# Products of constants in the waits of TensorE, in a two-block kernel on one core

## What is computed

```python
# first block: 16 experts of width 512, each row goes to its best two
g_idx = top_k(softmax(xt @ rg_w + rg_b), 1)          # router 1
v, e_idx = top_k(expert logits of that group, 2)
y += comb[:, e:e+1] * ((silu(xt @ e_gate[e]) * (xt @ e_up[e])) @ e_down[e])
x = rms_norm(x + y, norm_f_g)                        # the join of the two blocks

# second block: 16 experts of width 2048, each expert picks its best 64 rows
probs = softmax(h @ w_router); gate, idx = top_k(probs.T, 64)     # router 2
xs = h[idx]                                          # gather
y = (silu(xs @ w_gate) * (xs @ w_up)) @ w_down * gate
out = rms_norm(x + segment_sum(y, idx), final_g)
```

## Time and profile before

| | us |
|---|---|
| median of 3 runs | 2079.98 (2079.97 to 2083.10) |
| profiled execution, its own time | 2081.55 |
| span of the profiled execution, first to last instruction | 2080.1 |
| TensorE busy in the span | 1863.6 (90%) |
| VectorE, ScalarE busy | 491.8, 272.3 |
| mean granted clock of TensorE | 0.965 |

### The profile page before, as it was taken

The page is one execution under the profiler, slowest core; times in us unless marked ns, Lnnn a source line. Parts: engine busy times, 40 slices in busy tenths (PEclk is TensorE's granted clock), DMA queues, the critical chain, the costliest instruction groups (busy, mean ns, idle before and its releaser), DMA issues.

```text
span 2080.1 us, 19253 instructions
## 1 busy us (share of the span) xinstructions
PE 1863.6 (90%) x8342; PEld 750.9 (36%) x8342; DVE 491.8 (24%) x978; ACT 272.3 (13%) x478; POOL 33.9 (2%) x44
## 2 busy tenths in 40 slices
PE   8999999979999969999995999988888888888886
PEld 4444444443333325545443333322222223222222
DVE  3566001241001026990124011111011111110112
ACT  3322000121010114402201100000000000000001
POOL 0000000010000010000000000000000000000000
PEclk9999999979999989999997999999999999999999
DMA  6221032456998881211256899999999999999996
GB/s 235 81 81 41 0 121 81 179 192 259 387 389 348 372 304 68 82 41 61 95 212 263 328 428 428 428 428 427 428 427 428 427 428 428 428 428 427 427 428 278
DMA packets 68537, 589.80 MB, mean 284 GB/s; under 512 B 5472, under 2 KB 6880, under 8 KB 37216
## 3 DMA queue, kind: packets, MB, share of 16 engines
q1 hardware_dynamic: 59904, 556.55, 64.8%
q10 hardware_dynamic: 4448, 17.28, 2.1%
q0 software_dynamic: 4096, 14.68, 2.1%
HBM read 575.91 MB, written 12.58 MB: 283 GB/s over the span
## 4 chain that ended last, share of the span: by engine, by line
PE 55%; DMA 36%; DVE 6%; issue 2%; ACT 1%; SPq 0%; POOL 0%; ACTq 0%; DVEq 0%
PE ps L252 23%; DMA ring<-in_w_up 21%; DMA ring<-in_w_down 9%; PE ps L2175 8%; PE ps L1032 7%; DMA ring<-in_exp_w_up 5%; PE ps L2201 5%; PE ps L661 3%; PE ps L1820 3%; PE ps L261 2%; PE ps L583 1%; PE ps L1712 1%; PE ps L2157 1%; DMA AR<-h_rows,AR 1%; PE ps L276 0%
## 5 line engine op out<-in xcount | busy, mean ns | idle before, releaser
L252 PE MATMUL ps<-AR,ring 128*128 128x512 f32 x1160 | 503.3, 595 | 4.9 <-DVE AR L2033 3.6
L252 PEld LDWEIGHTS ps<-AR,ring 128*128 128x128 f32 x1160 | 220.5, 191 | 280.7 <-issue 275.9
L2175 PE MATMUL ps<-ring,AR 128*64 128x512 f32 x1008 | 233.5, 607 | 43.8 <-DMA ring<-in_w_up 32.0
L1032 PE MATMUL ps<-ring,AR 128*32 128x512 f32 x1536 | 257.9, 623 | 12.6 <-DMA ring<-in_exp_w_up 10.0
L2313 DVE TENSOR_TENSOR XT<-XT,ps 128x512 f32<-128x512 f32 x128 | 82.0, 684 | 785.0 <-PE ps L2157 785.0
L2175 PE MATMUL ps<-AR 128*64 128x512 f32 x1040 | 235.2, 597 | 33.1 <-DMA AR<-in_w_up 23.5
L1032 PE MATMUL ps<-AR 128*32 128x512 f32 x768 | 164.2, 593 | 0.0
L2175 PEld LDWEIGHTS ps<-ring,AR 128*64 128x64 f32 x1008 | 69.1, 138 | 205.2 <-issue 119.7
L2175 PEld LDWEIGHTS ps<-AR 128*64 128x64 f32 x1040 | 71.6, 136 | 188.8 <-issue 120.7
L2201 PE MATMUL ps<-ring,AR 128*64 128x512 f32 x512 | 122.9, 628 | 6.7 <-DMA ring<-in_w_down 5.9
L1032 PEld LDWEIGHTS ps<-ring,AR 128*32 128x32 f32 x1536 | 72.5, 114 | 140.8 <-issue 140.3
(11 more groups left out here) (350 smaller groups left out, 1040.1 us busy)
## 6 DMA issues: line engine op xcount, KB each, us to landing
AR<-in_w_gate SPq DMA_DIRECT2D x33, 2048.0 KB, 33.6
ring<-in_w_up SPq DMA_DIRECT2D x32, 2048.0 KB, 35.4
AR<-in_w_up SPq DMA_DIRECT2D x32, 2048.0 KB, 33.5
ring<-in_w_down SPq DMA_DIRECT2D x32, 2048.0 KB, 35.4
AR<-in_w_down SPq DMA_DIRECT2D x32, 2048.0 KB, 35.4
ring<-in_w_gate SPq DMA_DIRECT2D x31, 2048.0 KB, 33.9
ring<-in_w_in SPq DMA_DIRECT2D x15, 2048.0 KB, 8.3
ring<-in_exp_w_up SPq DMA_DIRECT2D x15, 2048.0 KB, 13.7
```

What stands on the lines that cost most here:

```text
L252: x = PE.matmul(ps, l, r, start=i == 0, stop=i == len(pairs) - 1)
L1032: yield k, c, PE.matmul(b[32 * c:32 * c + 32, :], rows(k), w(k), start=k == 0, stop=k == nk - 1, tile_position=(0, 32 * c), skip_group_che ...
L2175: x = PE.matmul(GU[2 * m + f // 2][64 * (f % 2):64 * (f % 2) + 64, :], XS[n // 2 % 2][:, k * P + 64 * b:k * P + 64 * b + 64], w[:, kk_, f ...
```

## The change

A helper `idle_products(ps, n)` is added. It runs n products of the identity by 384 columns of constants into a PSUM bank. Nobody reads the result, and the bank's next user overwrites it. The helper is called at five places of TensorE's program, with 3, 7, 8, 14 and 7 products. No wait, no other engine's work and no load is changed.

```diff
+        def idle_products(ps, n):
+
+            for i in range(n):
+                PE.matmul(ps[:, 0:384], ident, con[:, 0:384], start=True, stop=True)
@@ pe_front
             for h in range(2):
                 gain_rows("gf", h, bank[x_bank(6 + h)])
 
+            idle_products(bank[x_bank(4)], 3)
             PE.wait_ge(s_rv, V_MSK)
@@ pe_few
             index(0)
             index(1)
+            idle_products(bank[f_bank["r1", 0]], 7)
             rows(0)
@@ pe_mixer2
+            idle_products(bank[7], 8)
             turn(0)
@@ pe_choice
             x.then_inc(s_cp, 1)
+            idle_products(DN, 14)
 
             PE.wait_ge(s_cv, V2_IF)
@@ pe_choice
             PE.wait_ge(s_cv, V2_ID)
+            idle_products(DN, 7)
             rows(0)
```

## The result

| | before | after |
|---|---|---|
| median of 20 runs each | 2080.29 us (2078.26 to 2083.10) | 2073.96 us (2068.13 to 2082.87) |
| ratio, 95% interval | | 0.9969 [0.9962, 0.9977] |
| profiled execution, its own time | 2081.55 | 2073.95 |
| span | 2080.1 | 2072.6 |
| mean granted clock | 0.965 | 0.977 |

The ratio, taken from the means, says that the change makes the kernel 0.31% or 6.4 us faster (4.8 to 7.9 by the interval); the medians are 6.3 us apart. The forecast was 2074.0.

A forecast was written before the change was run, and what follows sets the result against it. The last stream of loads waits for TensorE to free a slot, so TensorE time won before 1186 us counts. Gains of 2.8 and 3.2 us, 6.0 off the 2079.98 us median, give 2074.0 us, range 2071.3 to 2078.5.

The forecast's parts named there:

- The sum: Gains of the five calls added: 0 + 2.8 + 0 + 0 + 3.2 = 6.0 us.
- What bounds the kernel: Last load stream, after a hole, waits for TensorE to free a slot; only TensorE time won before 1186 us counts.
- The cost of a product: Each 384-column product takes 0.65 us at full clock, 1.30 at half; the clock rises after 4.4 to 5.2 us.
- 3 products before the mask: Hidden by TensorE's wait before the mask, with little gained behind: 0 us, bounds 0 to 0.4.
- 7 at the first gather: Before the first block's rows(0): 3.28 us of faster work less 0.5 of lateness, 2.8 us won.
- 8 at the join: They end about 3 us before turn(0), likely losing the clock again: 0 us, bounds 0 to 2.0.
- the join's case: Rival: turn(0) at the join runs at full clock, winning 2.0 us more, 2072.0 us; chance 0.07.
- 14 at the second router: After its transposes, hidden by 1 us in the wait for VectorE: 0 us, perhaps full clock for the next call.
- 7 at the second gather: Before the second block's rows(0): 3.47 us of faster work less 0.3 of lateness, 3.2 us won.
- The clock falls again: Rival: clock lost between filler and dense products at one or both gathers, 2076.2 to 2078.8 us; chance 0.15.
- Nothing: Rival: the products do nothing for the clock, or their gain is taken up elsewhere: 2080 us; chance 0.10.
- Slower: Rival: the clock doesn't rise and the products outlast their waits, 10.9 us lost, 2090.9 us; chance 0.05.

The follow-up runs named there:

- e1: Changed kernel with only the 7 products ahead of the first block's rows(0), the other four calls removed: 2076.38 us, ratio 0.9976.
- e2: Changed kernel with only the 7 products ahead of the second block's rows(0), the other four calls removed: 2077.39 us, ratio 0.9982.
- e3: Changed kernel with only the two calls of 7 products, one at each gather: 2075.57 us, ratio 0.9975.
- e4: Changed kernel with only the 14 products after the second router's transposes: 2079.45 us, ratio 0.9993.
- e6: Changed kernel with products of 16 instead of 384 columns, same calls and places: 2079.68 us, ratio 0.9998.
- e11: Changed kernel measured once more, no edit: 2074.53 us, ratio 0.9976.
- e5: Changed kernel with 14 instead of 8 products at the join: 2070.52 us, ratio 0.9952.
- e9: Changed kernel plus 2 products ahead of up_a in pairs 2 to 7 of the first block's experts: 2067.14 us, ratio 0.9935.
- e7: Changed kernel with 14 products at the join, plus 4 before the first norm's sums and 5 before the second mixer's second ga tile: 2070.64 us, ratio 0.9949.
- e8: Changed kernel with 28 instead of 14 products after the second router's transposes: 2077.05 us, ratio 0.9988.
- e10: Changed kernel plus 2 products before up_a (pairs 2 to 7), 4 before the first norm, 14 at the join, 9 at the second gather: 2065.45 us, ratio 0.9929.

## Why the prediction was right, and where it wasn't

**The sum.** 6.0 us were forecast and 6.4 measured (4.8 to 7.9). That the median came within 0.1 us of the forecast is luck: the two places give 2.9 + 2.6 = 5.5 us over all traces, and what nobody changed moves by more than the difference, as the points show.

**What bounds the kernel.** Right. All 7.5 us of the profile are won ahead of the load that closes the hole; behind it 878.30 and 878.31 us.

**The cost of a product.** Right: at full clock 14 instructions take 4.78 us, 0.68 a product against the estimated 0.65. The rise took 4.3 and 5.1 us after the start, and 3.9 to 5.4 over all traces of the wide filler at the gathers, near the 4.4 to 5.2. It doesn't hold at the join: without filler the clock rose 4.4 us after `turn(0)` started in the trace of before, and 7.9 to 9.5 us after in e1, e2, e3, e4 and e6. "Every dense stretch in the rows rose within 5.2 us" was right for the rows of one trace only.

**3 products before the mask.** 0, as forecast, as far as it can be told: e1 and e3, without them, have 22.00 and 22.10 us at the first gather, the seven traces with them 21.91 to 22.52. The forecast had the clock full when they start; in the profile after it had fallen at 443.2 us, before them, and was back at 446.6.

**7 at the first gather.** 2.85 us in the profiles against 2.8, 2.9 over thirteen traces. The faster work behind the filler is worth 3.29 us against the forecast's 3.28. The 0.5 us of lateness is the lucky part: the filler was not late in the profile after, but the gathered rows landed 0.44 us later than in the profile before (11.62 against 11.18 us after the mask). In the six traces where the filler ended last, `rows(0)` came 0.05 (e1) to 0.7 us (e11) later than in the profile of before.

**8 at the join.** The reason was right: they end too early, and `turn(0)` took 3.42 us against the "close to 3.77". The stage of the join won 0.87 us in the profiles, within the bounds of 0 to 2.0, and 0 over all traces. e5 shows what the forecast called the join's case when the filler reaches to the work; there it is worth 3.1 us, more than the 2.0 that the row of before gave. The forecast took it that a gap of 3 us would cost the clock: here it was 3.5 us long and did cost it, 3.0 us in; but e5's clock held over 3.58 us at the gating. Such a gap may go either way.

**14 at the second router.** They were hidden by 1.1 us against the 1 forecast, and brought nothing alone (e4). The full clock for the next call, which the forecast hoped for, was there in the profile after and gone in e5, e9 and e11.

**7 at the second gather.** Forecast 3.2 us, in the profiles 1.70 + 2.55 = 4.25, and another 1.70 at the down instructions, where the fall of the earlier trace rows is gone; over all traces 2.6. Two terms of the step were off in size. The 0.3 us of lateness wasn't there in this trace, because the 14 had left the clock high, and the gather landed 1.0 us sooner (6.72 us after the index products against 7.69); in e11, of the same kernel, the filler was last and `rows(0)` came after 8.43 us. And the 2.59 us were too much: the first 64 instructions take 15.4 to 16.9 us in the four traces without filler (mean 16.1) and 14.15 on the mean of the nine with it, which is 1.9 us. The trace of before was the slowest of the four over the whole place, so the profile's gain of 5.95 is more than twice what the place gives on the mean. The forecast's 3.2 lies between the two.

**What the forecast left out.** Stretches in which nothing was changed moved by -0.35, +0.83 and +1.63 us. Falls of the clock at other places move such stretches, and the third is one of them. Before router 2 there are 16 instructions of 512 columns whose chain rows are, in the profile before and after,

```profile
1108.38 6.98 PE ps L1820 x16
```

```profile
1105.08 8.67 PE ps L1828 x16
```

1.69 us apart, and up to their start the stage differs by 0.07 us only. The clock fell here in ten traces, whose stage takes 312.5 to 312.9 us; in before and e5 it didn't, and the stage takes 311.11 and 310.85; in e7 it fell earlier in the stage, at 896.5 us (312.53). In the experts, five falls cost some 8 us (see e9), but before and after have five each, so they don't explain the +0.83, which stays without a cause. The range took in some of this by the three runs' 3.1 us; the changed kernel's 20 runs span 14.7 us.

**The rivals.** *The clock falls again*: not in the profile after (7.06 and 13.95 us), but once in e7 (15.55). The Trainium skill, "TensorE: Matmul & The Clock Gate", Part 4 (PE-mode transpose), has it that transposes don't count as busy for the clock in the way that products do. By that rule the prediction had both gains lost; the traces don't bear out so much, for in nearly all of them the clock holds over 1 to 2 us of transposes. With one of the two gains lost the prediction's own prices give 2076.2 to 2076.6, not "about 2077". *The join gains too*: it can, with 14 (e5). *Nothing*: this is what narrow products give (e6). *Slower*: e8, with twice the filler, moved that way, by 4.0 us, though still under the kernel before.

**What stays open.** Why the changed kernel spreads so much (14.7 us against 4.8 in 20 runs each, though the kernel before has 10.5 us in 34 others). Its slow runs have the lower granted clock: 0.971 to 0.976 in the four slowest of the 20, 0.979 to 0.981 in the four fastest. So falls of the clock have a part in it; which ones, only traces of such runs could tell. e9, e10 and e5 spread by 4 to 7 us in five runs each, which is too few to tell. And whether the gains of the two gathers add up fully (e1 and e2 against e3).

## What to carry to other kernels

A wait of TensorE costs more than its length when the clock falls in it: look behind each wait on the chain for the same group of instructions at two durations (9.28 and 7.08 us here), and price the filler by that difference. Unread wide products in the wait won it back where they ran right up to the work: 7 instead of none ahead of a gather, 14 instead of 8 at the join; too many cost directly (28 instead of 14: 4 us). Look for short waits inside loops as well: two products ahead of six of the `up_a` won as much again as all five calls of the change, or more (ratio 0.9935 against 0.9969 and, on the same chip, 0.9976). And take several traces of the kernel before: its one profile was the best of six at the join and the worst of four at the second gather.

## What the runs showed of the hardware

- Instructions alone don't raise the clock: 78 of 16 columns left it at 0.50 over the first gather (e6), the same number of 384 columns at the same places raised it (profile after).
- The clock also falls inside nearly dense work. In the first block's experts (95% busy) it did so five times in the trace of before, at 1.7 us each, and never in e9. TensorE idles there for 1.6 to 1.9 us only, behind 1.4 us of transposes and small products.
- A gap of about 3 us does not decide the matter. After 2.8 us of idling it had fallen at the first gather of before, after 3.0 us at the join of the profile after; it held over 3.58 us at the gating in e5, where eleven other traces lost it around the end of a gap of 2.8 to 3.6 us.
- The gather of rows was faster where the weight loads had ended: at most 5.52 us from the index products to the rows beside 179 GB/s (e8), 6.72 beside 398 GB/s (profile after) and 7.0 to 7.7 in six other traces. That is one trace against seven.
- Traces differ by 3.3 us in one place where none of them has wide filler: from the index products to the 17th down instruction before, e1, e4 and e6 took 51.08, 48.01, 49.59 and 47.77 us. A gain read off one pair of profiles carries that error.
